# Identity matrix loaded by itself behind the first token tile, the other constants with the second set, and three token tiles scaled ahead of the columns' products

## What is computed

```python
def encoder_step(x, states, params):
    ...
        mix, (hr, hi, C, n, m) = mixer(rmsnorm(x, norm_mix[l]), ...)     # S5 and mLSTM branches, gated and merged
        x = x + mix
        ff = moe(rmsnorm(x, norm_moe[l]).reshape(bsz * L, D_MODEL), ...)  # best 4 of 32 experts
        x = x + ff.reshape(bsz, L, D_MODEL)
    y = rmsnorm(x, norm_final)
```

## Time and profile before

| | us |
|---|---|
| median of 3 runs | 1305.03 |
| lowest and highest of them | 1304.78, 1305.94 |
| the profiled execution | 1302.26 |
| its span, first to last instruction | 1300.5 |

### The profile page before, as it was taken

How to read it: one execution, slowest core, us unless ns; L and a number is a source line. 1 busy time by engine, 2 the same in 40 slices (tenths; PEclk the granted TensorE clock), 3 DMA queues, 4 the chain that set the end, 5 groups by cost and what they waited for, 6 DMA issues and landing times.

```text
span 1300.5 us, 22589 instructions
## 1 busy us (share of the span) xinstructions
PE 1244.7 (96%) x7932; PEld 565.4 (43%) x7933; DVE 466.5 (36%) x923; ACT 169.7 (13%) x299; POOL 254.3 (20%) x444
## 2 busy tenths in 40 slices
PE   7999998999599999999999999999999999999996
PEld 4666666667433333343333333433333333333332
DVE  6757757231732222232222222322222223222224
ACT  4741015112300000000000000000000000000002
POOL 1157750000421111112111111121111111211100
PEclk9989999999699999999999999999999999999999
DMA  8323332497379999999999999999999999999995
GB/s 224 98 66 98 98 97 72 138 321 291 146 306 422 421 421 422 422 422 422 422 422 422 423 422 422 423 422 422 423 422 422 422 422 422 422 422 422 422 422 216
DMA packets 97120, 440.89 MB, mean 339 GB/s; under 512 B 16100, under 2 KB 45312, under 8 KB 47936
## 3 DMA queue, kind: packets, MB, share of 16 engines
q1 hardware_dynamic: 94720, 439.31, 83.8%
q10 hardware_dynamic: 2368, 1.15, 0.3%
HBM read 437.97 MB, written 1.87 MB: 338 GB/s over the span
## 4 chain that ended last, share of the span: by engine, by line
PE 79%; DVE 9%; DMA 5%; ACT 3%; SPq 2%; issue 2%; POOL 0%; DVEq 0%; POOLq 0%; ACTq 0%
PE psum L830 32%; PE psum L868 16%; PE psum L493 13%; PE psum L810 7%; DMA big<-in_w_gate_up_dram 4%; PE psum L749 3%; PE psum L471 2%; SPq L369 2%; DVE m L1659 2%; DVE m L1662 2%; DVE m L1656 2%; ACT m L1128 1%; PE psum L505 1%; PE psum L840 1%; PE psum L592 1%
## 5 line engine op out<-in xcount | busy, mean ns | idle before, releaser
L830 PE MATMUL psum<-big,m 128*64 128x512 f32 x2048 | 473.1, 597 | 1.9 <-DVE m L1639 1.2
L1646 DVE TENSOR_TENSOR acc<-acc,psum 128x512 f32<-128x512 f32 (+1 forms) x192 | 123.1, 682 | 572.5 <-PE psum L810 572.5
L830 PEld LDWEIGHTS psum<-big,m 128*64 128x64 f32 x2048 | 137.6, 136 | 303.0 <-issue 282.7
L868 PE MATMUL psum<-big,m 128*64 128x512 f32 x1024 | 226.8, 595 | 0.0
L493 PE MATMUL psum<-big,m 128*128 128x320 f32 x576 | 165.4, 442 | 2.7 <-DVE big L1288 1.0
L1245 POOL COPY m<-uT 96x64 bf16 x32 | 7.5, 234 | 675.1 <-PE psum L854 674.8
L493 PEld LDWEIGHTS psum<-big,m 128*128 128x128 f32 x576 | 108.5, 193 | 53.9 <-issue 12.7
L868 PEld LDWEIGHTS psum<-big,m 128*64 128x64 f32 x1024 | 71.3, 137 | 134.2 <-issue 129.5
L810 PE MATMUL psum<-m 64*128 64x512 f32 (+1 forms) x384 | 106.7, 632 | 0.0
L1128 ACT ACTIVATE m<-m 128x512 f32<-128x512 f32 x32 | 20.2, 632 | 580.4 <-DVE m L1656 580.4
L796 PE MATMUL psum<-m 128*128 128x64 bf16 x2376 | 76.8, 195 | 5.6 <-POOLq L1241 5.6
(11 more groups left out here) (258 smaller groups left out, 826.3 us busy)
## 6 DMA issues: line engine op xcount, KB each, us to landing
big<-in_w_gate_up_dram SPq DMA_DIRECT2D x256, 1024.0 KB, 21.7
big<-in_w_down_dram SPq DMA_DIRECT2D x128, 1024.0 KB, 23.4
m<-in_w_in_dram SPq DMA_DIRECT2D x18, 1024.0 KB, 5.3
m<-in_w_s_glu_dram SPq DMA_DIRECT2D x8, 512.0 KB, 4.4
m<-in_w_out_dram SPq DMA_DIRECT2D x4, 1024.0 KB, 10.9
acc<-in_x_prompt_dram SPq DMA_DIRECT2D x4, 512.0 KB, 5.1
m<-in_w_ml_out_dram SPq DMA_DIRECT2D x2, 1024.0 KB, 5.0
out_dram<-acc SPq DMA_DIRECT2D x2, 512.0 KB, 2.7
```

Source lines behind the costliest of these rows:

```text
L830: mm = pe.matmul(psum[SLOT * hf:SLOT * hf + SLOT, GB + gu, :], xeT[:, c, :], big[:, base:base + 512], start=(c == 0), stop=(c == GU_CHUNKS ...
L868: mm = pe.matmul(psum[SLOT * hf:SLOT * hf + SLOT, DB, :], hT[:, m, half, :], big[:, base:base + 512], start=False, stop=(c == DN_CHUNKS - ...
L1646: v.tensor_tensor(x, x, psum[0:n, CB + hf, :], ALU.add).then_inc(S("added"), 1)
```

## The change

SyncE issues the identity alone (128 rows of 512 bytes, 64 KB) right behind tile 0, under the old semaphore. The other 416 columns that are kept (208 KB) are issued behind weight group 2, ahead of the second constants and of the wait for the memset, and count on the second constants' semaphore; so both who wait for that one (TensorE behind projection 2, GpSimd ahead of the padding) wait for 32 instead of 16. On VectorE `scaled(2)` moves from between the products of tiles 0 and 1 to right behind `scaled(1)`, ahead of the wait for the vectors.

```diff
             for i, (t0, n) in enumerate(TILES):
                 sp.dma_start(acc[0:n, i, :], x_rows[i]).then_inc(S(f"x_landed{i}"), 16)
-            sp.dma_start(cst[:, :], a["consts"][:, 0:C_KEEP]).then_inc(S("cst_landed"), 16)
+                if i == 0:
+                    sp.dma_start(ident, a["consts"][:, C_ID:C_ID + P]).then_inc(S("cst_landed"), 16)
...
                 if g == 2:
 
+                    sp.dma_start(cst[:, P:C_KEEP], a["consts"][:, P:C_KEEP]).then_inc(S("cst2_landed"), 16)
                     sp.wait_ge(S("wg_zero"), 1)
                     sp.dma_start(cst2, a["consts"][:, C_KEEP:C_ALL]).then_inc(S("cst2_landed"), 16)
...
                 if j == 2:
-                    pe.wait_ge(S("cst2_landed"), 16)
+                    pe.wait_ge(S("cst2_landed"), 32)
...
             pool.wait_ge(S("cnat_landed"), 32)
-            pool.wait_ge(S("cst2_landed"), 16)
+            pool.wait_ge(S("cst2_landed"), 32)
...
-            scaled(0)
-            scaled(1)
+            for i in range(3):
+                scaled(i)
             dve.wait_ge(S("vcT"), 1)
             v.tensor_copy(vc[:, :], psum[:, 0, 0:16]).then_inc(S("vc_ready"), 1)
             dve.wait_ge(S("vc_ready"), 1)
             for i, (t0, n) in enumerate(TILES):
-                if i == 1:
-                    scaled(2)
                 dve.wait_ge(S("xT"), i + 1)
```

## The result

The changed kernel takes 1307.15 us (median of 20 runs, 1304.95 to 1309.91) against 1304.95 for the kernel before (20 runs, 1303.41 to 1307.83): a ratio of 1.0016, 95% interval 1.0009 to 1.0022. It is 0.16% slower, where 0.07% faster was forecast, and it lies above the range. Its profiled execution took 1309.36 us with a span of 1307.6, 7.1 us over the one of before.

A forecast was written before the change was run, and what follows sets the result against it. TensorE and DMA were taken as full in the expert loop, which starts when earlier stages end. First projection 0.86 us earlier (1.05 less 0.19 push), later constants free: 1305.03 - 0.86 = 1304.2 us, range 1302.6 to 1306.6.

The forecast's parts named there:

- part 1's price: Identity issued behind tile 0 pushes tile 2's square on ScalarE by 0.19 us by bytes; ends 0 and 0.57.
- The first rival: The push eats the gain: tile 2 lands late and VectorE can't start vc before it; 1305.0 us, chance 0.14.
- point of no gain: The push of tile 2 that leaves nothing gained: 1.05 us, giving 1305.0 us.
- The vectors: Transfers L376 to L378, wanted by TensorE behind tile 0 at 8.67 us; coming at 9.59 would cost 0.71 us.
- The clock, worse: TensorE's clock falls at L575, L578 or is low at the first projection: 2.9 us more, 1307.1; chance 0.09.
- theory K: From the experiments' expectations: TensorE pauses ahead of the first projection, and its half clock there carries the loss on.
- TensorE starts with tile 0's scaling: With the identity landed early, TensorE's first transposes start at 6.77 us instead of 7.69, gaining 0.92 us.
- The sum of part 2: VectorE scales tile 2 ahead of vc and products; first projection moves from 13.97 to 12.92 us, 13.11 with push.
- Part 3: Other 208 KB of constants issued behind the third weight group: costs nothing, covers 1.5 and 2.1 us.
- what is lost in front passes to the end: The expert loop starts when earlier stages end, so a microsecond won or lost ahead passes through one to one.

The follow-up runs named there:

- e6: Kernel before plus an unused 64 KB transfer of 16 rows of 4 KB between tiles 0 and 1; ratio 1.0020.
- e9: Kernel before plus an unused transfer of one 4 KB row between tiles 0 and 1; ratio 1.0014.
- e14: Kernel before with SyncE waiting for GpSimd's second memset between tiles 0 and 1, no transfer added; ratio 1.0016.
- e1: The changed kernel again, unaltered; ratio 1.0010 to the kernel before.
- e13: The kernel before again, unaltered; only a profiled execution and one time, 1306.54 us.
- e11: Changed kernel with the identity written on the chip by GpSimd (memset and select) instead of transferred; ratio 0.9990.
- e16: The same kernel as e11 once more, identity written by GpSimd; ratio 0.9987.
- e7: Kernel before plus an unused 64 KB transfer of 128 rows of 512 bytes between tiles 0 and 1; ratio 1.0024.
- e18: Changed kernel with the identity issued between tiles 1 and 2 instead of 0 and 1; ratio 0.9994.
- e17: e11 with VectorE in the old order, tile 2 scaled behind tile 0's product; ratio 0.9994.
- e8: Changed kernel with SyncE waiting for tiles 1 and 2 to land before issuing weight group 0; ratio 1.0005.
- e12: e11 plus 16 transposes of the identity on TensorE ahead of tile 0's; ratio 0.9996.
- e10: Changed kernel with the identity issued first, ahead of tile 0; ratio 1.0004.
- e3: Changed kernel with the identity issued behind all three tiles; ratio 0.9994.
- e15: The same kernel as e12 once more, only a profiled execution and one time; first two projections 8.88 us.

## Why the prediction was wrong

**The step that failed is part 1's price**: "I take 0.19 us as the push of that square ... the ends are 0 and 0.57." Measured against the same ScalarE instruction it is 9.53 - 7.12 = 2.41 us; against the second trace of the kernel before, which has it at 8.09, it is still 1.44. Both ends came from bytes and from issue; neither allowed for engines that are busy and slow, and the earlier trace rows had the hint, tile 2 taking 1.2 us longer than tile 1 at half its size. The first rival had the right mechanism (tile 2 late, VectorE waits on it, the gain is eaten) and the right point of no gain, 1.05 us, but I priced it just there, at 0.95 to 1.05, and so it gave 1305.0.

**The vectors** were bounded by 9.59 us as "as late as they can be", because in the old order the transpose of them started there. In the changed kernel they came at 10.19. It cost nothing here, since VectorE had only then to scale tile 2 and copied vc at 11.90. A bound taken from a row holds only as long as the queue ahead of it behaves as in that row.

**The Trainium skill's rule** in "DMA: Bandwidth & Descriptors", Rules for kernel authors, against small transfers pointed the right way. The 0.95 us for 64 KB in its Bandwidth section, a table of transfers issued from GpSimd, is far from the 2.41. And e6, e9 and e14 show that smallness was not the reason: large rows, 4 KB and no transfer at all cost about as much (1.0020, 1.0014 and 1.0016).

**The clock, worse** came true beside it, and not as an alternative; it had a chance of 0.09. The first two projections took 10.87 us (11.43 in e1) instead of 8.89. But e13, the kernel before, has 10.34, and e11 and e16, one kernel, have 10.57 and 8.88. So it is in part a draw for any version. The Trainium skill, "TensorE: Matmul & The Clock Gate", Part 1, says that the gate's window is free-running and does not reset when a kernel starts; these pairs agree with it in kind.

That the clock makes these projections long is shown by the packed traces' records of it. In the five traces with 8.88 us it is at full before the projection starts and stays there (in the kernel before from 11.84 us, projection at 13.97). In the other fifteen it rises only within the projections (18.04 us in e13, 19.12 and 20.31 in the changed kernel's two), or, in e11, falls at 13.68 and rises again at 17.10. What makes it rise late is open. Where tile 1 is late the long case is the rule, 10.5 us or more in nine of ten traces (e14 is the tenth); where it is in time six of ten have 10.3 to 10.6. TensorE's pause behind tile 0's transposes (theory K) is not needed for it: between those transposes and the projection e6, e7 and e9 pause for 0.47 and 0.78 us, no longer than the kernel before (0.47 and 1.02), and their projections take 10.5 to 11.9 us.

**What held.** TensorE starts with tile 0's scaling (6.67, forecast 6.77). The sum of part 2 held step by step where the landing let it, in e16, e11 and e18 (12.65, 12.73 and 12.74; forecast 12.92 with no push). Its value alone, about 0.5 us, is shown by e17. Part 3 cost nothing that the trace shows: in the changed kernel the b matrix's products (L1337) start 0.03 us after their columns' copy, and TensorE's gate_part has no wait. That what is lost in front passes to the end fits the traces: the changed kernel's two have s5_columns' transposes at 26.11 and 26.73 us, those of the kernel before at 23.00 and 25.54, on average 2.15 us apart, and the medians are 2.20 apart. Some of that match is luck, since the two of the kernel before are 2.54 apart by themselves. Of the 2.15 us only 0.6 stand ahead of the projection (15.10 and 15.17 against 13.97 and 15.05); the other 1.5 are the clock in it. How much of the clock's part the late landing brings is not shown.

**The range** was too narrow by the same step: with 2.4 us of push for 0.19 the forecast would have been 1305.03 - 1.05 + 2.41 = 1306.4. With the 1.5 us of clock on it, which the prediction had as a rival only, it is 1307.9, against 1307.15 measured; that is worked out afterwards and proves nothing.

## What to carry to other kernels

Whatever is put into the head of a transfer queue must be priced by when the next transfer that somebody waits for is then issued, not by the bytes put in: here 0.38 us later (e9) was 1.9 us at the next square, and one place further down the change's 64 KB were free (e18). A small constant that gates the first work need not be loaded at all if an engine that is idle then can write it: 0.9990 and 0.9987 here, the only ratios whose intervals lie below 1, though not clear of the 0.9994 with the transfer in a better place. And if a part of a change makes a chain depend on a transfer that had cover before, ask what its landing did in more than one execution: the two traces of the kernel before have tile 2's square at 7.12 and 8.09.

## What the runs showed of the hardware

- A tile's 4 KB rows took 160 ns each between 3.5 and 4 us in the kernel before, but the last ones of a late tile took 318 ns on average in the changed kernel and 337 in e8, where next to nothing else was moving. Such a tail followed the later issue of the second tile in nine of nine traces, and came once without it (e12).
- GpSimd writes a 128 x 128 identity in 0.20 + 0.29 us and TensorE starts on it 1.56 us after the start. The same 64 KB by transfer landed 1.9 us after their issue (e10, first in the queue), 4.0 (e18) or 5.4 (e3, behind all three tiles). From the timeline of e12 (columns as above):

```profile
0.77 0.20 POOL L1147 MEMSET cst<- 128x128 f32 x1 [0.29 <-POOLq L1707]
...
1.22 0.29 POOL L1149 TENSOR_SCALAR_AFFINE_SELECT cst<-cst 128x128 f32<-128x128 f32 x1 [0.25 <-POOL cst L1147]
```

- 3.67 us of transposes on TensorE from 1.56 us on did not leave it at full clock at 6.65, after a pause of 1.4 us; the eight transposes there took 1.97 us in both traces (e12, e15).
- The granted clock shows as 1.00 in the profile's column until the trace's first record of it, here at 10 to 22 us. Before that only durations tell: eight transposes took 1.97 us at 7.69 in the kernel before, and 1.09 at full clock.
- The same program's first two projections took 8.88 or 10.57 us, and the loop over the experts 939.6 to 942.2 us over all versions, of which none changes anything in it. So two single profiles of this kernel can't be compared to better than a few microseconds: the two of the kernel before have spans of 1300.5 and 1304.8 us.
